# The last down projection of a two-block layer stack, from its fifth row on, as pairs of 64-row matmuls in the two row halves of TensorE

## What is computed

```python
def rms_norm(x, g):
    x32 = x.astype(jnp.float32)
    y = x32 * lax.rsqrt(jnp.mean(x32 * x32, axis=-1, keepdims=True) + EPS)
    return y.astype(x.dtype) * g

def swiglu(x, w_gate, w_up, w_down):          # w_down: 2816 x 1024
    return (jax.nn.silu(x @ w_gate) * (x @ w_up)) @ w_down
...
        h = h + FFN_RES * swiglu(rms_norm(h, ffn2_norm[l]), ffn2_w_gate[l], ffn2_w_up[l], ffn2_w_down[l])
    return rms_norm(h, final_norm)
```

## Time and profile before

| what | value |
|---|---|
| median of 3 timed runs | 856.16 us (854.63 to 856.21) |
| profiled execution | 856.17 us, its span 854.4 us |
| TensorE busy | 822.6 us (96%), 6371 matmuls |
| VectorE busy | 561.1 us (66%) |
| ScalarE busy | 464.2 us (54%) |
| GpSimd busy | 125.5 us (15%) |
| last down projection (line 541) | 264 matmuls, from 788.9 us on |
| granted TensorE clock, whole span | 0.993 |

### The profile page before, as it was taken

One profiled execution on the slowest core, in us unless ns is written; L12 is line 12 of the kernel. 1 busy time (PEld: TensorE's weight loads), 2 busy tenths in 40 slices (PEclk: granted clock), 3 DMA queues, 4 the chain that ended last, 5 costly groups with the idle time before them and its releaser, 6 DMA issues.

```text
span 854.4 us, 16458 instructions
## 1 busy us (share of the span) xinstructions
PE 822.6 (96%) x6371; PEld 784.1 (92%) x6371; DVE 561.1 (66%) x817; ACT 464.2 (54%) x726; POOL 125.5 (15%) x143
## 2 busy tenths in 40 slices
PE   5999779999999999999999999999999999999997
PEld 5999779898689999999999998988999999999886
DVE  6988994876748766666447755365467766666443
ACT  5678544777747544445336455555556544444334
POOL 9325620213512100000003002000000300000000
PEclk9999989999999999999999999999999999999999
DMA  8624346363234766665654644344446576666561
GB/s 253 205 75 149 99 137 209 106 211 104 75 98 148 214 197 183 175 193 151 217 174 151 193 149 128 120 127 123 145 149 197 161 211 187 181 177 187 177 197 49
DMA packets 104105, 136.36 MB, mean 160 GB/s; under 512 B 5049, under 2 KB 92529, under 8 KB 104049
## 3 DMA queue, kind: packets, MB, share of 16 engines
q1 hardware_dynamic: 102288, 133.26, 51.7%
q0 software_dynamic: 1600, 2.28, 1.1%
q10 hardware_dynamic: 160, 0.05, 0.0%
HBM read 134.51 MB, written 1.05 MB: 159 GB/s over the span
## 4 chain that ended last, share of the span: by engine, by line
PE 81%; DVE 8%; ACT 5%; issue 3%; POOL 3%; DMA 1%; POOLq 0%; SPq 0%; DVEq 0%; ACTq 0%
PE bank L481 60%; PE bank L541 7%; PE bank L489 7%; POOL arena L433 2%; DVE w_lo L1370 2%; PE bank L739 2%; ACT a_hi L928 2%; ACT w_hi L928 2%; DVE arena L1545 1%; ACT arena L928 1%; PE bank L720 1%; DVE w_hi L1366 1%; PE bank L732 1%; PE bank L893 1%; PE bank L740 1%
## 5 line engine op out<-in xcount | busy, mean ns | idle before, releaser
L481 PE MATMUL bank<-a_hi,w_hi 128*128 128x256 f32 (+1 forms) x1672 | 479.4, 287 | 14.6 <-DVE w_lo L1370 9.8
L481 PE MATMUL bank<-a_lo,w_hi 128*128 128x256 f32 (+1 forms) x1672 | 474.9, 284 | 0.0
L481 PE MATMUL bank<-a_hi,w_lo 128*128 128x256 f32 (+1 forms) x1672 | 474.7, 284 | 0.0
L1370 DVE TENSOR_TENSOR w_lo<-stage,w_hi 128x1024 fp32r<-128x1024 f32 x250 | 319.0, 1284 | 226.5 <-ACT w_hi L928 226.2
L928 ACT ACTIVATE w_hi<-stage 128x1024 fp32r<-128x1024 f32 x244 | 255.0, 1053 | 173.7 <-PE bank L481 128.8
L481 PEld LDWEIGHTS bank<-a_hi,w_hi 128*128 128x128 f32 x1672 | 322.6, 193 | 21.1 <-issue 14.1
L481 PEld LDWEIGHTS bank<-a_lo,w_hi 128*128 128x128 f32 x1672 | 322.8, 193 | 0.0
L481 PEld LDWEIGHTS bank<-a_hi,w_lo 128*128 128x128 f32 x1672 | 322.7, 193 | 0.0
L928 ACT ACTIVATE arena<-arena 128x512 f32<-128x512 f32 (+4 forms) x63 | 38.0, 606 | 82.4 <-DVE arena L1437 42.9
L433 POOL TENSOR_TENSOR arena<-arena 128x512 f32<-128x512 f32 x12 | 23.0, 1926 | 391.6 <-ACT arena L928 391.3
L489 PE MATMUL bank<-w_hi,a_hi 128*128 128x256 f32 x208 | 60.5, 291 | 1.7 <-DVE a_lo L1405 1.7
(11 more groups left out here) (179 smaller groups left out, 684.5 us busy)
## 6 DMA issues: line engine op xcount, KB each, us to landing
stage<-ffn_w_gate SPq DMA_DIRECT2D x44, 512.0 KB, 4.0
stage<-ffn_w_up SPq DMA_DIRECT2D x44, 512.0 KB, 3.8
stage<-ffn_w_down SPq DMA_DIRECT2D x44, 512.0 KB, 3.6
stage<-w_in SPq DMA_DIRECT2D x40, 512.0 KB, 3.5
stage<-a_w_in SPq DMA_DIRECT2D x24, 512.0 KB, 4.8
stage<-b_w_in SPq DMA_DIRECT2D x16, 512.0 KB, 3.6
stage<-a_w_out SPq DMA_DIRECT2D x12, 512.0 KB, 4.3
stage<-b_w_out SPq DMA_DIRECT2D x8, 512.0 KB, 3.5
```

The lines of the kernel that those rows point to most:

```text
L481: mm = pe.matmul(dst, w[:, slot, c:c + P], a[:, k, :] if isinstance(k, int) else wide(a[:, bass.ds(k, 1), :]), start=start and n == 0, sto ...
L1370: dve.tensor_tensor(w_lo[:, n % RING, 0:w], src, w_hi[:, n % RING, 0:w].bitcast(F32), ALU.subtract)\
```

## The change

`LOWER = 12` names the first row that is done in the new way. For rows 8 to 11 nothing changes. From row 12 on each 128-row matmul becomes two of 64 rows: contraction rows 0 to 63 go into bank 0 to 3 as before, and rows 64 to 127 into bank 4 to 7, which start afresh with the first product of row 12. Ahead of row 12 TensorE waits until VectorE has emptied the last up bank (`ff_u`, `first + 11`).

At the end each result lies in two banks. ScalarE copies bank 4 + q to SBUF (`final_half`), VectorE adds bank q to that copy (`final_sum`), and the Square and the product with the gain read the sum from SBUF. Both now wait for `fin_sum`, no longer one for the other.

```diff
+LOWER = 12
...
             def row_by_token(half, k, tb, h):
 
                 slot, t, c = half % RING, slice(tb * P, (tb + 1) * P), slice(h * 512, (h + 1) * 512)
                 for w, a in ((w_hi, a_lo), (w_lo, a_hi), (w_hi, a_hi)):
-                    mm = pe.matmul(token_bank(tb, h)[:, :], a[:, k, t], w[:, slot, c], start=False, stop=w is w_hi and a is a_hi,
-                                   skip_group_check=True)
+                    last = w is w_hi and a is a_hi
+                    if k < LOWER:
+                        mm = pe.matmul(bank[2 * tb + h][:, :], a[:, k, t], w[:, slot, c], start=False, stop=last,
+                                       skip_group_check=True)
+                        continue
+                    for i, rows in enumerate((slice(0, HD), slice(HD, P))):
+                        mm = pe.matmul(bank[4 * i + 2 * tb + h][:, :], a[rows, k, t], w[rows, slot, c],
+                                       start=i == 1 and k == LOWER and w is w_hi and a is a_lo, stop=last,
+                                       skip_group_check=True)
                 return mm
...
                 for c in range(10):
                     pe.wait_ge(ff_lo, first + c + 1)
+                    if 8 + 2 * c == LOWER:
+                        pe.wait_ge(ff_u, first + 11)
...
+            def final_half(q):
+                act.wait_ge(fin_acc, q + 1)
+                f(tiles(16 + 2 * q, 2), bank[4 + q][:, :], ACT.Copy).then_inc(fin_half, 1)
+
             def final_square(q):
-                act.wait_ge(fin_acc, q + 1)
-                f(tiles(16 + 2 * q, 2), bank[q][:, :], ACT.Square, accum_out=fin_ms[:, q:q + 1]).then_inc(fin_sq, 1)
+                act.wait_ge(fin_sum, q + 1)
+                f(tiles(24 + 2 * q, 2), tiles(16 + 2 * q, 2), ACT.Square, accum_out=fin_ms[:, q:q + 1]).then_inc(fin_sq, 1)
...
+            def final_sum(q):
+                dve.wait_ge(fin_acc, q + 1)
+                dve.wait_ge(fin_half, q + 1)
+                dve.tensor_tensor(tiles(16 + 2 * q, 2), bank[q][:, :], tiles(16 + 2 * q, 2), ALU.add).then_inc(fin_sum, 1)
+
             def final_gained(q):
-                dve.wait_ge(fin_sq, q + 1)
-                dve.tensor_tensor(tiles(8 + 2 * q, 2), bank[q][:, :], fin_gain[:, (q % 2) * 512:(q % 2 + 1) * 512], ALU.mult)\
-                    .then_inc(fin_g, 1)
+                dve.wait_ge(fin_sum, q + 1)
+                dve.tensor_tensor(tiles(8 + 2 * q, 2), tiles(16 + 2 * q, 2), fin_gain[:, (q % 2) * 512:(q % 2 + 1) * 512],
+                                  ALU.mult).then_inc(fin_g, 1)
```

More of the change, by code:

```diff
@@ L236, in build @@
             sem(n) for n in ("br_done", "mg_a", "mg_b", "mg_f", "mg_hi", "mg_lo"))
-        fin_acc, fin_sq, fin_g, fin_bias, fin_std, fin_inv = (
-            sem(n) for n in ("fin_acc", "fin_sq", "fin_g", "fin_bias", "fin_std", "fin_inv"))
+        fin_acc, fin_half, fin_sum, fin_sq, fin_g, fin_bias, fin_std, fin_inv = (
+            sem(n) for n in ("fin_acc", "fin_half", "fin_sum", "fin_sq", "fin_g", "fin_bias", "fin_std", "fin_inv"))
         fin_gain_in, fin_a, fin_d, out_done = sem("fin_gain_in"), sem("fin_a"), sem("fin_d"), sem("out_done")
@@ L531, in row_half @@
                 mm.then_inc(ring_free, 1)
-            def token_bank(tb, h):
-                return bank[2 * tb + h]
             def row_by_token(half, k, tb, h):
@@ L549, in down_by_token @@
                     for q in range(4):
-                        pe.matmul(token_bank(tb, h)[:, q * P:(q + 1) * P], xres[:, 4 * h + q, tb * P:(tb + 1) * P], ident,
+                        pe.matmul(bank[2 * tb + h][:, q * P:(q + 1) * P], xres[:, 4 * h + q, tb * P:(tb + 1) * P], ident,
                                   is_transpose=True, start=q == 0, stop=False, skip_group_check=True)
@@ L1343, in final_scaled @@
                 f(y, y, ACT.Identity, scale=n_rstd[:, tb:tb + 1]).then_inc(fin_a, 1)
+            final_half(0)
+            final_half(1)
             final_square(0)
+            final_half(2)
             final_square(1)
             final_root(0)
+            final_half(3)
             final_square(2)
@@ L1974, in _ @@
             dve.wait_ge(fin_gain_in, 16)
[L1975 to L1979, removed]
+            for q in range(4):
+                final_sum(q)
+                final_gained(q)
+                if q % 2:
+                    final_bias(q // 2)
+                if q == 2:
+                    final_out(0)
+            final_out(1)
 _INS = ["x", "a_norm_g", "a_w_in", "a_conv_w", "a_conv_b", "a_gate_r_w", "a_gate_r_b", "a_gate_i_w", "a_gate_i_b",
```

## The result

The changed kernel takes **858.27 us** (median of 19 runs, 856.8 to 858.63) against 854.8 us (19 runs, 854.58 to 856.29) for the kernel before in the same comparison: a ratio of 1.003, 95% interval 1.0023 to 1.0037. It is slower, by 0.3%.

A forecast was written before the change was run, and what follows sets the result against it. TensorE's matmul rate in the last down projection, then a serial tail, was taken to set the end: 856.17 + 0 (pairs) + 0.09 (mode) + 2.0 (tail) = 858.3 us, range 855.7 to 862.5.

The forecast's parts named there:

- What bounds this stage: Last down projection: weights arrive in time; TensorE's pace through 264 matmuls of 512 columns, then a serial tail, sets the end.
- A pair costs what one matmul costs: Rows 12 to 29: 216 pairs at 227 ns replace 216 matmuls at 227 ns, so 0 us.
- The upper bound: Concurrent pairs step at most 227 + 7 = 234 ns, adding the members' gap of at most 0.01 us: +1.5 us.
- The mode: Going from 128-row to 64-row matmuls: one step of 0.21 us instead of 0.12, 0.09 us paid once.
- The wait for the up banks: Ahead of row 12: costs nothing, the last bank being empty at 788.11 and TensorE arriving at 799.87.
- The tail: After the last matmul: four unhidden ScalarE copies and four VectorE additions, +2.0 us, between 1.2 and 2.6.
- The late copy: In the tail, ScalarE's copy 3 runs only after root 0, 849.17 to 849.77, 0.15 us late.
- the late addition: In the tail, VectorE's addition 3 waits behind the first output product, 850.45 to 851.14, its copy ready at 849.8.
- The 0.40 us pause: Unexplained pause ahead of the first output product in the kernel before; a reason for taking +2.0 rather than 1.9 us.
- The sum: Whole kernel: 856.17 + 0 (pairs) + 0.09 (mode) + 2.0 (tail) = 858.3 us, with no correction for profiling.
- Rival A: Paired halves hide each other's fixed cost, the step falling from 227 towards 215 ns: 857.8 to 855.7 us; chance 0.30.
- Rivals B and C: B: halves take turns, 49 us more, 907 us, chance 0.10. C: partial collision, 234 to 260 ns, 860 to 866 us, 0.10.

The follow-up runs named there:

- lower_half_only: Changed kernel without the matmuls of contraction rows 64 to 127 of rows 12 to 29, and with the old kernel's end; 856.35 us in one run.
- pairs_256: Changed kernel with each pair of 512 columns split into two pairs of 256 columns; 861.44 us in one run.
- lower_8: Changed kernel with pairs from row 8, the projection's first, instead of row 12: 264 pairs, not 216; 856.75 and 858.20 us in the two groups.
- two_banks: Changed kernel with full 128-row matmuls instead of pairs, odd rows into banks 4 to 7, even into 0 to 3, same new end; 856.57 and 858.06 us.
- end_reordered: Changed kernel with only the order of ScalarE's and VectorE's work in its end altered, nothing added or removed; 856.57 and 858.11 us.

## Why the prediction was right, point by point

- **What bounds this stage.** Right: the projection is as long as TensorE's steps make it, and the weights wait for it in both traces.
- **A pair costs what one matmul costs (0).** Right: 227 ns before and after, with 48 or 216 pairs. The reason given, that each half pays its own fixed cost, is shown by lower_half_only (227 ns alone) and pairs_256 (120 ns). The upper bound added the members' distance to each step; they do start within 0.01 us of one another, but the step doesn't grow by it.
- **The mode, 0.09 us.** Mis-sized: the first step was right (0.32 instead of 0.227), but the second one, 0.33, comes with it. The two make 0.20 us, a few more steps of up to 0.24 the rest of the 0.24 us in all, and the earlier trace rows, which show only the first step, couldn't tell.
- **The wait for the up banks, 0.** Right, even when it is moved to the front (lower_8, empty 0.95 us ahead).
- **The tail, +2.0 us.** Right in size: 1.89 in the trace, 1.9 by two_banks. The walk gave 852.47 for the last scaling, it came at 852.56; counted from the last matmul's start, 3.87 walked and 3.83 seen. The late copy (849.17 walked, 849.25 seen) and the late addition (850.45 and 850.46) are there. The 0.40 us pause ahead of the first output scaling that I allowed for did not return. Of the tail's chain, end_reordered tests 0.2 us; that the rest is the copy and the addition one behind the other is read from the rows, and fits the 1.9 us of two_banks.
- **The sum, 858.3.** Met by the median of 858.27, but that is partly luck. The sum was built on an upper-group execution, and its "no correction" overlooked that 854.63, 856.16 and 856.21 come from two groups; had the median of the changed kernel come from the lower one, it would have been 856.9, below the 857.9 to 860.4 of the forecast, though within the whole range of 855.7 to 862.5. The difference is the better test: +2.1 forecast, +2.2 measured in either group. In it two errors cancel in part: the mode was 0.15 us too cheap, the tail 0.11 too dear.
- **Rival A** is out: with or without a partner the step is 227 ns. Its "2 to 3 ns with float32" can't be read from the rows given: 0.22 us less 256 columns at 0.84 ns are 5 ns, and the view rounds to 10. The Trainium skill's 216 ns for a step of 512 columns (TensorE: Matmul & The Clock Gate, Back-to-back issue gap) was met by no float32r matmul here; they step at 227 ns.
- **Rivals B and C** are out: two full-rate streams ran together at 227 ns a pair. The Trainium skill's 4 ns for a further tile (TensorE: Matmul & The Clock Gate, Packing small matmuls) fits members less than 0.01 us apart; the step is no longer for it, 227 ns with a partner and without.

## What to carry to other kernels

Splitting a full contraction into two row halves moved the same columns through the array in the same time (227 ns a step); the fixed cost per matmul wasn't hidden by a partner, because each half paid it in its own stream. What the split does add is real: a second set of banks to join at the end, behind the last matmul where nothing covers it. A kernel whose times fall into groups needs its groups told apart before a difference of 0.3% is read. Read the step between starts and fit it over two sizes before working on such a cost, and price every operation behind the last matmul in full.

## What the runs showed of the hardware beyond that

- Two 64-row float32r matmuls in different halves ran at full rate together (227 ns a pair), and the halves kept independent lists: three matmuls of one half in turn cost nothing (projection 59.97 us), twelve cost 19.8 us, as the engine reached 3 to 4 matmuls ahead.
- Changing between 128-row and 64-row matmuls cost 0.24 us each time, both ways (24 changes, 5.7 us), most of it in two slow steps of 0.32 and 0.33 us.
- A step of float32r was its columns at 0.42 ns and about 12 ns on top (227 ns for 512 columns, 120 for 256), with 128 rows or as a pair of 64; one half alone took 227 ns too. What these 12 ns are stays open: no kernel here changed them.
- Times went by where a piece at 1.2 GHz fell: with the granted clock at 0.89 to 0.92 from 120 to 135 us a kernel took 1.5 us more than with 1.00, the unchanged one too, six times what the pairs cost.
